# MoE step on one core: expert rows scaled per slot and added into one sum in DRAM, routing without the large one-hot

## What is computed

```
x = x + g1 * rmsnorm(mix)                      # (1032, 1024), kept in DRAM as x1
h = modulate(rmsnorm(x))                       # expert input, 1032 rows of 1024
scores = sigmoid(h @ router_w)                 # (1032, 64)
idx = top 8 of 64 experts, out of the best 4 of 8 groups
w   = scores[idx] / sum(scores[idx]) * 2.5
routed[t] = sum over the 8 experts e of t:  w[t,e] * (silu(h@Wg[e]) * (h@Wu[e])) @ Wd[e]
shared[t] = (silu(h@Sg) * (h@Su)) @ Sd         # one expert that every token takes
y = x + g2 * rmsnorm(routed + shared)
```

## Time and profile before

| | us |
|---|---|
| median of 3 runs (2045.13 to 2049.24) | 2048.44 |
| the profiled execution, its own time | 2049.87 |
| its span | 2048.1 |
| TensorE busy | 1771.7 (87%) |
| VectorE busy | 1247.6 (61%) |
| ScalarE busy | 883.9 (43%) |
| GpSimd busy | 351.1 (17%) |

### The profile page before, as it was taken

One profiled execution on the slowest core, in us unless ns is written; L12 is line 12 of the kernel. 1 busy time (PEld: TensorE's weight loads), 2 busy tenths in 40 slices (PEclk: granted clock), 3 DMA queues, 4 the chain that ended last, 5 costly groups with the idle time before them and its releaser, 6 DMA issues. The chain is left out here.

```text
span 2048.1 us, 23996 instructions
## 1 busy us (share of the span) xinstructions
PE 1771.7 (87%) x7667; PEld 1205.8 (59%) x7668; DVE 1247.6 (61%) x1588; ACT 883.9 (43%) x1305; POOL 351.1 (17%) x330
## 2 busy tenths in 40 slices
PE   6968999967998898526999999999999999997863
PEld 1214454432335666426888888888888888883321
DVE  0124555645124555596777777777777777771888
ACT  0001111104234655204666676767676767671221
POOL 0004465640000000001111010101010101002453
PEclk9989999988999999758999999999999999999986
DMA  9934555557776211335799999999999999974686
GB/s 288 353 113 150 165 156 179 161 175 242 233 229 197 78 47 59 105 142 186 287 359 375 350 352 350 350 368 367 351 354 350 356 372 361 351 296 149 243 314 235
DMA packets 180374, 519.63 MB, mean 254 GB/s; under 512 B 23711, under 2 KB 65312, under 8 KB 154748
## 3 DMA queue, kind: packets, MB, share of 16 engines
q1 hardware_dynamic: 141075, 393.68, 54.7%
q0 software_dynamic: 23296, 67.66, 8.6%
q10 hardware_dynamic: 15892, 56.92, 7.0%
HBM read 423.50 MB, written 111.40 MB: 261 GB/s over the span
## 5 line engine op out<-in xcount | busy, mean ns | idle before, releaser
L1929 PE MATMUL ps<-hi_gu,xT_hi 128*128 128x512 f32 x768 | 309.3, 403 | 0.0
L1975 DVE TENSOR_TENSOR lo_gu<-raw_gu,hi_gu 128x1024 fp32r<-128x1024 f32 x256 | 304.1, 1219 | 0.5
L1929 PE MATMUL ps<-hi_gu,xT_lo 128*128 128x512 f32 x768 | 300.8, 392 | 0.0
L1929 PE MATMUL ps<-lo_gu,xT_hi 128*128 128x512 f32 x768 | 299.1, 390 | 0.0
L1859 ACT ACTIVATE hi_gu<-raw_gu 128x1024 fp32r<-128x1024 f32 x256 | 258.9, 1051 | 0.0
L562 PE MATMUL ps<-w_in_sb,hT 128*128 128x512 f32 (+1 forms) x576 | 252.9, 600 | 0.3 <-ACT hT L497 0.3
L1841 POOL DMA_INDIRECT xg<-h_d,tokb x96 | 96.0, 1000 | 779.7 <-PE ps L1915 769.8
L478 POOL TENSOR_TENSOR prod<-kring,qbc 128x512 f32<-128x512 f32 x128 | 164.6, 1319 | 282.3 <-DMA kring<-in_cache_k 232.1
L562 PEld LDWEIGHTS ps<-w_in_sb,hT 128*128 128x128 f32 (+1 forms) x576 | 103.4, 181 | 143.4 <-issue 143.0
L1979 DVE TENSOR_TENSOR xT_lo<-ps,xT_hi 128x1024 fp32r<-128x1024 f32 x96 | 117.6, 1225 | 87.8 <-ACT xT_hi L1865 87.8
L1929 PEld LDWEIGHTS ps<-hi_gu,xT_lo 128*128 128x128 f32 x768 | 144.4, 188 | 32.2
(11 more groups left out here) (309 smaller groups left out, 2603.1 us busy)
## 6 DMA issues: line engine op xcount, KB each, us to landing
raw_gu<-in_expert_w_gate SPq DMA_DIRECT2D x64, 1024.0 KB, 7.4
raw_gu<-in_expert_w_up SPq DMA_DIRECT2D x64, 1024.0 KB, 11.0
raw_dn<-in_expert_w_down SPq DMA_DIRECT2D x64, 1024.0 KB, 10.2
rows_d<-yb ACTq DMA_DIRECT2D x96, 512.0 KB, 8.8
kring<-in_cache_k SPq DMA_DIRECT2D x128, 256.0 KB, 2.9
vring<-in_cache_v SPq DMA_DIRECT2D x128, 256.0 KB, 3.0
rows_d<-zeros SPq DMA_DIRECT2D x64, 512.0 KB
adaw<-in_ada_w SPq DMA_DIRECT2D x12, 2048.0 KB, 10.6
```

Source lines behind the costliest of these rows:

```text
L1929: last = pe.matmul(ps[:, 2 + b % 2, :].rearrange("p (a f) -> p a f", a=2), x[b % 2][:, k, :], w[:, :, k * F:(k + 1) * F], start=(k == 0 an ...
L1975: dve.tensor_tensor(lo_cut(n, u), raw_cut(n, u), hi_cut(n, u).bitcast(F32), ALU.subtract).then_inc(lo_made, 1)
```

## The change

The result of each expert block is scaled by its slots' weights when it leaves PSUM, and added to one sum per token in DRAM (`acc_d`, 1032 x 1024) by an indirect transfer with an addition. Such a transfer is issued only when the one before it has landed. `rows_d`, its zero fill, its gathers and VectorE's weighted sums are gone.

- Routing: MATCH_REPLACE marks the top 8, and one comparison gives the mask. The weights are kept dense, `wd` = mask x score x 2.5 / sum, and stored as `wd_d` (1032 x 64). Destinations come from MAX8 over (place + 1) x mask.
- The shared expert of tiles 0 to 2 (`NWIN` = 3) is computed during routing, from weights loaded at the end of attention, and stored as the first content of `acc_d`; the rows of tiles 3 to 8 are set to zero. `EARLY` falls from 3 to 2.
- Main: GpSimd also gathers for each block 128 rows of `wd_d` (256 bytes each), picks the expert's column and issues the adding transfer of block b - 3. ScalarE's store is gone.
- Final: load `acc_d`, add the shared expert for tiles 3 to 8, norm, x1 (loaded ahead).

```diff
-EARLY = 3
+EARLY = 2
+NWIN = 3
@@ attention, SP, between load_x(NT - 2) and store_h2(NT - 3)
+                for m in range(2):
+                    sp.wait_ge(s_done[m], NI)
+                for h, w in enumerate((sw_gate, sw_up)):
+                    sp.dma_start(s_gu[:, h, :], w[0].rearrange("(p k) f -> p (k f)", k=KC)).then_inc(sw_in, 16)
+                sp.wait_ge(pv_done, NI)
...
@@ routing, VectorE
                 for t in range(T9):
-                    own(dve.max_index(top_i[:, t, :], top[:, t, :], sel[:, t, :]))
+                    own(dve.match_replace(left[:, t, :], top[:, t, :], sel[:, t, :], TAKEN))
                 own.wait()
-                do(dve.tensor_tensor(onehot[:, :, :], ...
-                do(dve.tensor_reduce(mask[:, :, :], onehot.rearrange("p (t k) e -> p t e k", k=TOPK), AX_X, ALU.add))
+                do(dve.tensor_scalar(mask[:, :, :], left[:, :, :], 0.5 * TAKEN, None, ALU.is_lt))
...
-                do(dve.tensor_tensor(pk, oh, sig[:, :, :].unsqueeze(2).to_broadcast([P, T9, TOPK, NE]), ALU.mult))
-                do(dve.tensor_reduce(wraw.rearrange("p t k -> p (t k)"), picked[:, :, :], AX_X, ALU.add))
+                dve.wait_ge(wd_made, 1)
+                do(dve.tensor_reduce(wsum[:, 0, :], wd[:, :, :], AX_X, ALU.add))
...
-                do(dve.tensor_tensor(pk, oh, tots[:, :, :].unsqueeze(2).to_broadcast([P, T9, TOPK, NE]), ALU.mult))
-                do(dve.tensor_reduce(dst_f[:, :], picked[:, :, :], AX_X, ALU.add))
+                do(dve.scalar_tensor_tensor(out=val[:, :, :], in0=tots[:, :, :], scalar=1.0, in1=mask[:, :, :], op0=ALU.add,
+                                            op1=ALU.mult))
+                for t in range(T9):
+                    own(dve.max(dst_k[:, t, :], val[:, t, :]))
@@ main stage, GpSimd
+                def slot_weight(b):
+                    r = rank_of(expert_of(b))
+                    e = pool.value_load(tbl[0:1, r:r + 1], min_val=0, max_val=NE - 1)
+                    pool.wait_ge(wr_in[b % 4], 16 * (b // 4) + 16)
+                    if b >= 4:
+                        pool.wait_ge(y_here, b - 3)
+                    pool.tensor_copy(wslot[b % 4][:, :], wr[b % 4][:, bass.ds(e, 1)]).then_inc(wslot_here, 1)
+
+                def scatter(b):
+                    pool.wait_ge(y_here, b + 1)
+                    if b:
+                        pool.wait_ge(rows_out[(b - 1) % 2], 16 * ((b - 1) // 2 + 1))
+                    pool.indirect_dma_start(out=acc_d[:, :],
+                                            out_offset=bass.IndirectOffsetOnAxis(ap=tokb[:, b:b + 1], axis=0),
+                                            in_=yb[b % 2][:, :], in_offset=None, bounds_check=NTOK - 1, oob_is_err=False,
+                                            compute_op=ALU.add).then_inc(rows_out[b % 2], 16)
...
+                for b in range(MAIN):
+                    if b + 2 < MAIN:
+                        gather(b + 2)
+                    slot_weight(b)
+                    if b >= 3:
+                        scatter(b - 3)
+                for b in range(MAIN - 3, MAIN):
+                    scatter(b)
@@ main stage, ScalarE
                     act.wait_ge(dn_mm, b + 1)
+                    act.wait_ge(wslot_here, b + 1)
...
-                                   ACT.Copy).then_inc(y_here, 1)
-
-                def store(b):
-                    act.wait_ge(y_here, b + 1)
-                    act.dma_start(rows_d[b * P:(b + 1) * P, :], yb[b % 2][:, :]).then_inc(rows_out[b % 2], 16)
+                                   ACT.Copy, scale=wslot[b % 4][:, 0:1]).then_inc(y_here, 1)
@@ final stage, VectorE
+                    if t in SH:
+                        u = t - NWIN
+                        dve.wait_ge(a0_in[t % A0], 16 * (t // A0) + 16)
+                        dve.wait_ge(dn6, u + 1)
+                        dve.tensor_tensor(y, ps[:, 4 + 2 * (u % 2):6 + 2 * (u % 2), :].rearrange("p b n -> p (b n)"), y, ALU.add
+                                          ).then_inc(summed, 1)
```

More of the change, by code:

```diff
@@ L2172, in _, with load_hidden @@
-                stores(fixed(7))
-                stores(fixed(8))
-                for j in range(2):
-                    sp.wait_ge(y_out[j], 16 * (NT // 2 + 1 - j) + 16)
-            @block.gpsimd
-            def _(pool):
-                own = Own(pool, pool5)
-                def gather(s, rows):
-                    wait(pool, summed, s.n - 1)
-                    own(pool.tensor_copy(didx[s.par][:, :], dst_i[:, bass.ds(s.n * TOPK, TOPK)]))
-                    own.wait()
-                    pool.sem_inc(didx_here, 1)
-                    for k in range(TOPK):
-                        pool.indirect_dma_start(out=rk[s.par][0:rows, k, :], out_offset=None, in_=rows_d[:, :],
-                                                in_offset=bass.IndirectOffsetOnAxis(ap=didx[s.par][0:rows, k:k + 1], axis=0)
-                                                ).then_inc(rk_in[s.par], 16)
-                gather(fixed(0), NS)
-                gather(fixed(1), P)
-                gather(fixed(2), P)
-                with own.loop(3, 2) as it:
-                    for s in (Step(2 * it + 3, 1, it + 1), Step(2 * it + 4, 0, it + 2)):
-                        gather(s, P)
+                def load_hidden(t):
+                    u = t - NWIN
+                    if u >= 2:
+                        sp.wait_ge(gu6, u - 1)
+                    sp.dma_start(hx2[u % 2][:, :, :], h2T_d[t].rearrange("p (k t) -> p k t", k=KC)).then_inc(hx2_in[u % 2], 16)
@@ new lines, in _ @@
+                load_hidden(NWIN)
+                load_hidden(NWIN + 1)
+                load_sums(0)
+                sp.dma_start(g2s[:, :], mod_d[0:NS, G2 * D:(G2 + 1) * D]).then_inc(g2s_in, 16)
+                load_sums(1)
+                load_sums(2)
+                for t in range(T9):
+                    if t in SH and t + 2 < T9:
+                        load_hidden(t + 2)
+                    store(t)
+                    if t + 3 < T9:
+                        load_sums(t + 3)
+                for j in range(A0):
+                    sp.wait_ge(y_out[j], 16 * ((T9 + A0 - 1 - j) // A0))
@@ L2216, in _ @@
-                gated(fixed(0), NS)
-                gated(fixed(1), P)
-                gated(fixed(2), P)
-                norm(fixed(0), NS)
-                with act.Fori(0, 2) as it:
-                    for s in (Step(2 * it + 1, 1, it), Step(2 * it + 2, 0, it + 1)):
-                        gated(s.next.next, P)
-                        norm(s, P)
-                for n in (7, 8):
-                    gated(fixed(n), P, more=False)
-                    norm(fixed(n - 2), P)
-                norm(fixed(7), P)
@@ L2308, in _ @@
-                total(fixed(0), NS)
-                hidden(fixed(2), P)
-                total(fixed(1), P)
-                finish(fixed(0), NS, g2s[:, :])
-                with own.loop(3, 2 * 9) as it:
-                    for s in (Step(2 * it + 2, 0, it + 1), Step(2 * it + 3, 1, it + 1)):
-                        hidden(s.next, P)
-                        total(s, P)
-                        finish(s.last, P, g2)
-                total(fixed(8), P)
-                finish(fixed(7), P, g2)
```

545 lines of the change are left out of this document (342 added, 203 removed).

## The result

The changed kernel takes 2064.46 us (median of 10 runs, 2060.2 to 2073.09) against 2048.23 us before (10 runs, 2043.18 to 2056.42): ratio 1.008, 95% interval 1.0061 to 1.0099. It is slower by 0.8%, where 1956 us was forecast. The profiled execution took 2073.09 us, with a span of 2071.3.

A forecast was written before the change was run, and what follows sets the result against it. TensorE was taken to bound the main stage; 2048.1 - 10 (routing) + 2 (shared weights' load, small things) + 7 (end of main) - 91.6 (final stage) = 1955.5 us, say 1956; own range 1940 to 1975, widened to 1938 to 2090.

The forecast's parts named there:

- the bound becomes TensorE: Final stage: VectorE's weighted additions go, TensorE sets the pace, 86.7 us instead of 178.3, 91.6 us less.
- The end that I gave for a low clock: Final stage: if TensorE stayed at half clock, its later products double, 57 us back.
- I cost the main stage at nothing: Main stage: TensorE's path is unchanged and additions land in 8 us, so 0 us change.
- cover is 9.34 us less the landing time: Main stage: margin before additions time the blocks; each microsecond over it costs 96 us.
- rival (2): Main stage: additions just time the blocks, landing in 9.4 to 10.2 us, total 1965 to 2040 us; chance 0.06.
- The lower bound of 4.2 us: Main stage: least landing time of an addition, from a gather of the same rows with empty queues.
- lighter queues: Main stage: without stores and zeros, three blocks' queue load falls from 27.6 to some 25 us, favouring an 8 us landing.
- The landing of 13.0 us, my upper bound: Main stage: slowest expected addition, the loaded gather's extra 4.4 us counted twice because an addition reads both sides.
- Routing, 4 us: Routing: earlier mask, counts and one-hots, partly given back to shared-expert work, first gather 10 us earlier; ends 0 and 20.
- Rival (3): Routing: TensorE's shared work and the late store eat the whole gain, total 1966 us; chance 0.06.
- The serial additions: End of main stage: the last three additions run in series, 7 us more; ends 0 and 15.
- Rival (1): Main stage: additions land later than 9.34 us on average and time it, costing 217 to 351 us; chance 0.20.

The follow-up runs named there:

- experiment 1: Changed kernel with a buffer for each of the final stage's six hidden tiles, all loaded at its start: 2014.29 us, ratio 0.9844.
- experiment 5: Changed kernel with both six hidden-tile buffers and two alternating sums in DRAM: 1968.95 us, ratio 0.9611.
- experiment 4: Changed kernel without the small gathers of slot weights and most column copies, results scaled by a constant: 2059.28 us, ratio 1.0054.
- experiment 3: Changed kernel whose indirect transfer stores its rows instead of adding them, still one at a time: 2019.41 us, ratio 0.9859.
- Experiment 7: experiment 1 with only one shared-expert tile in routing, eight tiles and eight hidden buffers in the final stage: 2021.13 us, ratio 0.9876.
- experiment 2: Changed kernel with blocks adding in turn into two sums, each addition waiting for the one two blocks before: 2024.32 us, ratio 0.9883.
- Experiment 10: experiment 9 with the nine x1 loads issued in the last stage behind the first sums: 1979.44 us, ratio 0.9665.
- experiment 9: experiments 8 plus gate and up of the first two hidden tiles worked before the main stage's barrier: 1966.62 us, ratio 0.9606.
- experiments 8: experiment 5 with the six hidden tiles loaded before the main stage ends: 1968.34 us, ratio 0.9621.
- 11: experiment 9 with ScalarE's and VectorE's last-stage lists putting the first hidden tiles ahead of the norms: 1959.75 us, ratio 0.9561.
- experiment 6: experiment 2's two sums, but each addition waits until the one before has landed: 2073.49 us, ratio 1.0139.

## Why the prediction was wrong

**The final stage, the largest miss** (54 of the 116 us between the forecast's 1955.5 and the span of 2071.3). The step that failed is "the bound becomes TensorE", with no wait but TensorE's. The price was right: 86.7 us forecast, 90.9 in experiment 1 and 90.1 in experiment 5, at about 12 us a tile (11.3). What was not done was to walk each engine's list. All that was needed stood in the diff: the order of `load_hidden`, `store` and `load_sums` on SP, with two buffers. The loop through them is 5.6 + 9.2 + 3.7 us of load and TensorE's products and some 5.6 of transposes, ScalarE, VectorE and hand-over for one tile. An estimate of it could have been made before the run from the prediction's own terms: 4.5 us for a load, 7.03 + 3.70 + 0.51 + 0.52 us of TensorE and its hand-over the earlier trace rows, and up to 7 us for addition, norm, scaling and x1 are up to 23 us a tile. The end that I gave for a low clock (57 us back) came near the miss of 54 us by luck. The low clock itself cost 2.2 us of the 12.9 us that a tile lost (a product of 9.2 instead of 7.03 us, tiles 24.2 instead of 11.3 us apart), and it came with the waiting: without it (experiment 1) the clock was at 1.00.

**The main stage, 49 us.** The step that failed is "I cost the main stage at nothing", on a landing of 8 us whose "cover is 9.34 us less the landing time". Two terms were off. The landing was 9.1 us in the mean and 9.3 in the median, not 8. And the 0.85 us from a landing to the next issue was put at nothing: the cover is 9.34 less landing and hand-over, so that 8 us would have left 0.5 us, and 9.1 us left none. The mechanism was seen and priced: each microsecond over the threshold costs 96 us, and 0.51 us cost 49. By its period of 9.85 us this is rival (2), 9.4 to 10.2 us, to which I gave 0.06; by its landing alone it would have been under that rival's threshold. Its times, 1965 to 2040 us, took the forecast's short final stage for granted. The lower bound of 4.2 us, a gather's, was fair: the shortest additions landed after 5.1 us here and 4.3 us in experiment 4. The 96 blocks hold 8256 rows, 86 of 128 slots on average; how far the landing follows from how full a block is was not looked at. The "lighter queues" were true (q1's 51.5%, and in the main stage a DMA share of 0.85 instead of 0.90) and did not help. What an addition costs the engines is read from GpSimd's queue, which holds gathers, additions and small rows; first experiment 3, without the addition, then experiment 4, without the small rows:

```profile
q0 software_dynamic: 30720, 69.81, 9.1%
```

```profile
q0 software_dynamic: 27648, 67.69, 13.4%
```

The changed kernel's 13.9% are 288 us, these are 184 and 276 us. The same 33.8 MB of results thus take 104 us more when they are added, and the small rows 12 us. Of the 184 us that leaves 172 for gathers and plain stores. If each takes half, as each of the two equal streams of gathers before took half of 176 us, it is 86 for the stores, against 190 for the additions: an estimate of 2.2 times. By the half rate that the Trainium skill, Collectives: The Full Stack, section "The bandwidth ceiling", gives for the reduction of a ReduceScatter it would be 2, and the trace is near that. The landing of 13.0 us, my upper bound, is not there: the engines' time for these bytes doubled, but the median landing is 9.3 us where the gather's was 8.6.

**Routing, 4 us.** Nearly right, and by its own steps: mask at 875.0 (873 forecast), the counts taken 14.8 us earlier in the stage (14), the loop of one-hots starting 21.9 us earlier (21). Then loop and end took 42.2 us instead of 28.2, 14 us back where I had 11, for VectorE waited 5.55 us for TensorE in its fourth tile. To the barrier 7.9 us were gained (10 forecast); the first gather then landed after 9.2 us instead of 7.4. Experiment 7 gives the parts: without tiles 1 and 2 routing is 22 us shorter than before, and the two give back 16.4. Rival (3), that nothing is gained here, was not right: 5.8 of 10 us came.

**End of main, 8 us.** The serial additions were forecast, and the 14.6 us lie within the ends of 0 and 15, just. What no step had was GpSimd's drain of 5.57 us behind the last transfer.

**Up to routing.** +3.1 us, but this is not shown to be the change. Routing's first row of ScalarE lies between 852.6 and 859.6 us over the changed kernel and the eleven experiments, which all run the same code up to there. The first 850 us differ by more from profile to profile.

Rival (1), that additions time the main stage, was the right mechanism at 49 us instead of 217 to 351. Alone it would not have turned the sign, had the final stage been as forecast (experiment 1: 2014 us with the main stage still slow). Nor would the final stage alone (experiment 2: 2024 us). It took both: with both removed, experiment 5 comes to 1969 us, 13 us over the forecast. The result lies inside the range, which had been widened for it, and outside the forecast's own 1940 to 1975.

**Still open.** An addition's 9.3 us under load was not taken apart further, and additions of fewer rows were not tried. What the 0.85 us from a landing to the next issue consist of is open too, and whether a hidden load in another place of SP's list would do with two buffers. Why two sums, with two transfers under way, gained only 1.5 us at the end of main is read from the profile alone: GpSimd's wait for the last addition ends 9.5 us after its issue in experiment 2 and 10.5 in experiment 5, beside the x1 loads, where the changed kernel's took 6.6. Experiment 10 took these loads away, and it landed 3 us earlier than in experiment 9.

## What to carry to other kernels

Before a stage is called bound by one engine, walk every queue's list once round the loop, the loads' queue first: here, with two buffers, a load that stood behind a store was timed by the store's whole chain. A transfer that waits for its predecessor is a serial chain. Its landing and the hand-over to the next issue (0.85 us here) must together lie under the period, with room for the late ones, and if they do not, a second destination (two sums, each waited for two blocks later) removes the wait for a few microseconds elsewhere. When an edit takes work off the path and nothing comes back, as in experiments 8 and 9, read what the next engine in the list is waiting behind; the gain came only when the lists were put in the order of need.

## What the runs showed of the hardware

- GpSimd's drain after its last indirect transfer took 5572 ns, the same in ten profiles (the changed kernel, experiments 1, 2 and 5 to 11), 5003 ns without the small gathers and 6920 ns with plain stores. What sets it was not tried. It costs only where it stands on the path.
- Issuing an adding transfer keeps GpSimd for 1.55 us at the quiet end and 1.62 us in the main stage, a gather 0.99 us. A plain scatter took 0.96 us at the end but 1.66 us in the main stage, and an addition 2.42 us there with two under way (experiments 2 and 9). With two sums but one addition at a time (experiment 6) it was 1.62 us again, so the second one under way goes with the longer issue, not the second sum.
- From the landing of an addition to the issue of the one that waits for it 0.85 us passed, in the changed kernel as in experiments 1, 4, 6 and 7 (medians).
- A stage with gaps is paid twice. With 11 us of waiting before each tile, TensorE's granted clock was 0.79 on average in the final stage, between its levels of 1.2 and 2.4 GHz, and a gate and up product took 9.2 us; without gaps it was 1.00 and 7.03 us.
